# Choosing experts in two batches, with two tiles' rows computed by ScalarE and GpSimd

## The reference

```
x = x + merged @ w_out
t = rms_norm(x, norm_ffn_g)
g_logits = t @ w_router_group + b_router_group          # 4 groups
g_sel = argmax(g_logits);  g_w = softmax(g_logits)[g_sel]
e_logits = (t @ w_router_expert + b_router_expert)[g_sel]   # 4 experts in the group
top_v, top_i = top_k(e_logits, 2);  top_w = softmax(top_v) * g_w
for e in range(16):                                     # combine: the two weights, else 0
    hid = silu(t @ w_gate[e]) * (t @ w_up[e])           # 1024 -> 512
    y += combine[:, e] * (hid @ w_down[e])
return final_rms_norm(x + y)
```

## Time and profile before

| What | Value |
|---|---|
| median of 3 runs | 842.87 us (841.27 to 843.12) |
| the profiled execution's own time | 843.01 us |
| its span, first to last instruction | 841.2 us |
| granted TensorE clock, mean | 0.993 |
| TensorE busy | 819.5 us of the span |
| from the last product of w_out to the first product of the experts | 513.95 to 535.46 us |

### The profile page before, as it was taken

How to read it: one execution, slowest core, us unless ns; L and a number is a source line. 1 busy time by engine, 2 the same in 40 slices (tenths; PEclk the granted TensorE clock), 3 DMA queues, 4 the chain that set the end, 5 groups by cost and what they waited for, 6 DMA issues and landing times.

```text
span 841.2 us, 15813 instructions
## 1 busy us (share of the span) xinstructions
PE 819.5 (97%) x5363; PEld 747.1 (89%) x5363; DVE 589.1 (70%) x957; ACT 512.4 (61%) x935; POOL 88.4 (11%) x77
## 2 busy tenths in 40 slices
PE   9999999999999999999999999999999999999992
PEld 8999999999999998999998888888888888888881
DVE  7383233687778767466457126899989999989995
ACT  7344214567666656554634233588888888888884
POOL 0000000000000000000000001122233322223112
PEclk9999999999999999999999999999999999999997
DMA  8541222233123312332335745799999999999924
GB/s 250 123 146 57 79 68 74 68 109 89 45 81 108 86 44 92 105 99 75 101 101 195 265 165 188 254 371 376 380 375 372 364 371 365 368 366 368 345 69 192
DMA packets 135817, 163.02 MB, mean 194 GB/s; under 512 B 18584, under 2 KB 103704, under 8 KB 135772
## 3 DMA queue, kind: packets, MB, share of 16 engines
q1 hardware_dynamic: 129674, 149.53, 52.7%
q0 software_dynamic: 5952, 12.82, 5.4%
q10 hardware_dynamic: 146, 0.07, 0.0%
HBM read 151.09 MB, written 20.12 MB: 204 GB/s over the span
## 4 chain that ended last, share of the span: by engine, by line
PE 53%; DVE 3%; DMA 2%; issue 1%; ACT 1%; POOLq 0%; POOL 0%; ACTq 0%
PE ps L1767 15%; PE ps L1769 15%; PE ps L1768 15%; PE ps L2219 2%; PE ps L2131 1%; DMA xg<-sum_rows,idi 1%; PE ps L2138 1%; PE ps L2241 1%; DMA sum_rows<-yb,ydn 1%; PE ps L2123 0%; PE ps L2164 0%; PE ps L2165 0%; PE ps L2062 0%; DVE wl L1153 0%; PE ps L1990 0%
## 5 line engine op out<-in xcount | busy, mean ns | idle before, releaser
L1642 DVE TENSOR_TENSOR wl<-rawM,wh 128x1024 fp32r<-128x1024 f32 x189 | 223.9, 1219 | 14.4 <-ACT wh L989 14.2
L989 ACT ACTIVATE wh<-rawM 128x1024 fp32r<-128x1024 f32 x192 | 195.6, 1055 | 6.7 <-PE ps L1769 3.7
L1767 PE MATMUL ps<-hTh,wh 128*128 128x272 f32 (+2 forms) x440 | 129.2, 294 | 1.5 <-ACT qkv L813 1.0
L1769 PE MATMUL ps<-hTh,wl 128*128 128x272 f32 (+2 forms) x440 | 127.4, 290 | 0.0
L1768 PE MATMUL ps<-hTl,wh 128*128 128x272 f32 (+2 forms) x440 | 126.8, 288 | 0.0
L1767 PE MATMUL ps<-wh,xh 128*128 128x256 f32 (+1 forms) x384 | 124.7, 325 | 0.3 <-DVE xl L1688 0.3
L1769 PE MATMUL ps<-wh,xl 128*128 128x256 f32 (+1 forms) x384 | 122.0, 318 | 0.0
L1768 PE MATMUL ps<-wl,xh 128*128 128x256 f32 (+1 forms) x384 | 122.0, 318 | 0.0
L1767 PE MATMUL ps<-wh,hTh 128*128 128x384 f32 x256 | 90.0, 352 | 0.2 <-DVE mA L1273 0.2
L1769 PE MATMUL ps<-wh,hTl 128*128 128x384 f32 x256 | 86.4, 337 | 0.0
L1768 PE MATMUL ps<-wl,hTh 128*128 128x384 f32 x256 | 86.2, 337 | 0.0
(11 more groups left out here) (331 smaller groups left out, 1715.0 us busy)
## 6 DMA issues: line engine op xcount, KB each, us to landing
rawM<-in_w_expert_up SPq DMA_DIRECT2D x64, 512.0 KB, 10.1
rawM<-in_w_expert_down SPq DMA_DIRECT2D x64, 512.0 KB, 8.6
rawM<-in_w_expert_gate SPq DMA_DIRECT2D x64, 512.0 KB, 9.0
rawA<-in_w_in SPq DMA_DIRECT2D x64, 192.0 KB, 3.1
rawA<-in_w_in SPq DMA_DIRECT2D x20, 512.0 KB, 5.3
rawA<-in_w_attn_branch SPq DMA_DIRECT2D x8, 512.0 KB, 3.5
rawA<-in_w_out SPq DMA_DIRECT2D x8, 512.0 KB, 4.3
x<-in_x_prompt SPq DMA_DIRECT2D x4, 512.0 KB, 6.0
```

Source lines behind the costliest of these rows:

```text
L989: nc.scalar.activation(wh[:, (c + 1) % S, :], rawM[:, slot, :], ACT.Copy).then_inc(m_hi, 1)
L1642: V.tensor_tensor(wl[:, sl, :], rawM[:, slot, :], wh[:, sl, :].bitcast(F32), ALU.subtract).then_inc(m_lo, 1)
L1767: T.matmul(out, sh, mh_, start=start, stop=False, **kw)
L1769: return T.matmul(out, sl, mh_, start=False, stop=stop, **kw)
```

## The change

Tiles 0 to 2 in order (AHEAD = 3) are now chosen as soon as their logits are there, while TensorE still works on the last two steps of w_out; the last two tiles follow as a second batch, in the same functions with a slice of tiles. `picked` is an array of its own. The position products of the second batch get a PSUM place of their own, and four products that carry the first batch's counts over run ahead of the second choice. The lists' products are split the same way. New waits go with it: the last two logits products wait until VectorE has read what is in their bank (`lg_read`), `place` of the first batch waits for the last square (item_hot has moved into that space), and the two last tiles' rows take another way: ScalarE scales them (`scale_rows`, after `scale_done`), then GpSimd multiplies with the gain, and stores them. The IDLE counts change, and two operations of `tail_lists` move ahead, the rest of it behind the first split rows.

```diff
-        IDLE = (3, 2, 24, 8, 5, 0, 9)
+        IDLE = (0, 2, 12, 3, 5, 0, 9)
...
@@ GpSimd, for each tile i @@
+                if i >= AHEAD:
+                    pool.wait_ge(scaled_done, i - AHEAD + 1)
+                    pool.tensor_tensor(hb[:, i % 2, :], hb[:, i % 2, :], gb[:], ALU.mult).then_inc(h2_done, 1)
                 pool.wait_ge(h2_done, i + 1)
...
@@ ScalarE @@
+            def scale_rows(i):
+                act.wait_ge(scale_done, i - AHEAD + 1)
+                act.wait_ge(y_out[i % 2], 16 * (i // 2))
+                nc.scalar.activation(hb[:, i % 2, :], x[:, ORDER[i], :], ACT.Copy, scale=rsx[:, i:i + 1]).then_inc(scaled_done, 1)
...
+                if s == 2 * NT - 2:
+                    scale_rows(AHEAD)
             m_hi_split(2, 0, 2, 0, first=True)
+            scale_rows(NT - 1)
...
@@ VectorE @@
+            add_half(NT + 2)
+            normal_rows(1)
+            m_lo_split(0)
+            normal_rows(2)
+            add_half(NT + 3)
+            dve.wait_ge(lg_mm, NT + AHEAD)
+            finish_logits(ahead)
+            select(ahead)
+            row_scale(AHEAD)
+            m_lo_split(1)
+            dve.wait_ge(lg_mm, 2 * NT - 1)
+            finish_logits(slice(AHEAD, NT - 1))
+            add_half(NT + 4)
+            list_values(ahead)
+            dve.wait_ge(ach, 3 * NT)
+            place(ahead, 0)
             row_scale(NT - 1)
...
-            normal_rows(NT - 1, scaled=True)
...
+            select(late)
+            list_values(late)
+            place(late, 1)
...
+            for part, ts in enumerate((ahead, late)):
+                ins = V.scalar_tensor_tensor(out=keep[:, ts], in0=positions[part][:, :, EXPERTS - 1], scalar=float(P),
+                                             in1=picked[:, ts, EXPERTS - 1], op0=ALU.is_lt, op1=ALU.mult)
...
-            tail_lists()
...
             m_lo_split(2)
+            tail_lists()
...
@@ TensorE @@
+                if s >= 2 * NT - 2:
+                    pe.wait_ge(lg_read, s - 2 * NT + 3)
...
+            lists(slice(0, AHEAD), 0)
             idle_products(IDLE[2], 2, *chunk)
...
+            lists(slice(AHEAD, NT), 1).then_inc(ls_mm, 1)
```

More of the change, by code:

```diff
@@ L246, in build @@
         order = r5("order", [P, NT, EXPERTS])
+        picked = r5("picked", [P, NT, EXPERTS])
         assert r5.pos[0] <= 203 * K, r5.pos[0]
@@ L1521, in _ @@
             dve.wait_ge(gb_in, 32)
[L1522 to L1537, removed]
+            gl, el = lg[:, :, 0:EG], lg[:, :, EG:20]
@@ new lines, in place @@
+            def place(ts, part):
+                n = ts.stop - ts.start
+                dve.wait_ge(pos_mm, part + 1)
+                pos = positions[part].unsqueeze(1).broadcast_to([P, 2, n, EXPERTS])
+                c, k_, j_, g_ = chosen[:, :, ts, :], pk[:, :, ts], pj[:, :, ts], ge[:, :, ts, :]
+                link(V.tensor_tensor(c, c, pos, ALU.mult))
+                link(V.tensor_reduce(k_, c, AX.X, ALU.add))
+                link(V.tensor_tensor(g_[:, :, :, 0:4], kt(k_, 4), row(C_STEP, 4, n), ALU.is_ge))
+                link(V.tensor_reduce(j_, g_[:, :, :, 0:4], AX.X, ALU.add))
+                link(V.scalar_tensor_tensor(out=k_, in0=j_, scalar=float(-P), in1=k_, op0=ALU.mult, op1=ALU.add))
+                link(V.tensor_tensor(g_, kt(j_, TILE_COLS), row(C_TILE, TILE_COLS, n), ALU.is_equal))
+                V.tensor_tensor(item_hot[:, :, ts, 0, :], kt(g_[:, :, :, 0], EXPERTS), oht[:, :, ts, :], ALU.mult)
+                for k in range(2):
+                    ins = V.tensor_tensor(slot_hot[:, k, ts, :], pk[:, k, ts].unsqueeze(2).broadcast_to([P, n, P]),
+                                          cst[:, C_SLOT:C_SLOT + P].unsqueeze(1).broadcast_to([P, n, P]), ALU.is_equal)
+                    ins.then_inc(hot_done, 1)
@@ L1559, in _ @@
[L1559 to L1564, removed]
@@ L2172, in _ @@
                     logits_half(s - 1)
+            ones, tri = cst[:, C_ONE:C_ONE + P], cst[:, C_TRI:C_TRI + P]
+            flat = picked[:].rearrange("p t e -> p (t e)")
+            position = ps[:, 6, 192:192 + AHEAD * EXPERTS]
+            position_late = ps[:, 0, 0:(NT - AHEAD) * EXPERTS]
+            es = lambda first, last: slice(first * EXPERTS, last * EXPERTS)
+            more = dict(skip_group_check=True)
+            pe.wait_ge(sel_done, 1)
+            T.matmul(position, tri, flat[:, es(0, AHEAD)], start=True, stop=False, **more)
+            for d in range(1, AHEAD):
+                ins = T.matmul(position[:, es(d, AHEAD)], ones, flat[:, es(0, AHEAD - d)], start=False, stop=d == AHEAD - 1, **more)
+            ins.then_inc(pos_mm, 1)
             idle_products(IDLE[0], 2, *chunk)
@@ L2186, in _, with lists @@
-            ins.then_inc(pos_mm, 1)
+            for first, last, to in ((1, 3, 0), (2, 3, 0), (0, 2, 0), (0, 1, 1)):
+                T.matmul(position_late[:, es(to, to + last - first)], ones, flat[:, es(first, last)], start=first == 1, stop=False, **more)
+            def lists(ts, part):
+                for k in range(2):
+                    pe.wait_ge(hot_done, 2 * part + k + 1)
+                    for t in range(NT)[ts]:
+                        ins = T.matmul(ps[:, 5, 0:FIRST], slot_hot[:, k, t, :], item_hot[:, k, t, 0, TAIL:],
+                                       start=(part == k == t == 0), stop=(k == 1 and t == NT - 1))
+                return ins
```

112 lines of the change are left out of this document (59 added, 53 removed).

## The result

The changed kernel takes 856.91 us (median of four runs, 852.72 to 857.88); the kernel before, run beside it, 842.61. The ratio is 1.0163, with a 95% interval of 1.0132 to 1.0193: slower by some 14 us, where 849.0 with an upper end of 853.4 was forecast. The profiled execution took 856.53 us, its span is 854.7 us. Three executions took 856.5 to 857.9 us at a mean granted clock of 0.978 or 0.979, one 852.72 us at 0.984.

The account below looks back on a forecast made before the run. VectorE's serial chain ahead of the experts was taken to bound the kernel. 843.0 - 0.7 (schedule) + 4.1 (GpSimd holding VectorE) + 2.7 (code switch) = 849.1, so 849.0 us, slower; range 843.9 to 853.4.

Parts of the forecast that it names:

- What bounds the kernel, and where: Router stage ahead of the experts: VectorE's serial chain decides when the experts start, and everything behind moves with them.
- VectorE's schedule, -0.7: Router stage: choosing in two batches leaves a smaller late batch, so the first expert product comes about 0.7 us earlier.
- Exclusion, +4.1: Router stage: GpSimd's two multiplications each hold a two-input VectorE operation, +2.0 and +2.1 us; bounds 0 and 5.2.
- The duration estimated at 2.2 us: Each GpSimd multiplication of 128x1024: 1.30 for a broadcast plus 0.88 for a second input; bounds 0.9 and 2.7 us.
- Rival (1): Only the code switch at the start costs; GpSimd's multiplications run beside VectorE: 844.9 us, chance 0.22.
- (2): Only GpSimd's holding of VectorE in the router stage costs, the code switch being quick: 846.3 us, chance 0.14.
- (3): GpSimd multiplies beside VectorE and the switch is hidden, so the second batch's shorter tail decides: 842.2 us, chance 0.19.
- The code switch, +2.7: Program start: GpSimd's code switch makes broadcast and first tile 3.4 us late, about 0.7 absorbed; bounds 0 and +7.1.
- The 7 us: Length taken for GpSimd's code switch, between transfer landings at 6.0 and 8.1 us; bounds 1.4 and 11.4 us.
- The 6 us switch with its 1.7 us: Range's lower end: a 6 us code switch alone, costing 1.7 us at the start, gives 843.9 us.
- Rival (4): Router stage: TensorE's clock falls between 514 and 520 us; 12 idle products 2.8 us longer, 1.1 hidden; no own chance.
- Fewer idle products cost nothing by themselves: Router stage: 12 idle products at 0.23 us are 2.8 us and end at 523, ahead of the second choice.

Follow-up runs that it names:

- mixed kernel: Changed kernel, one-column GpSimd broadcast added late in the experts, TensorE's gaps filled with idle products, some of them between the small products: 846.30 us, ratio 1.0043.
- code put back: Changed kernel plus one more GpSimd partition broadcast of a single column, read by nobody, late in the experts: 850.83 us, ratio 1.0090.
- the two experiments: Kernel before plus a one-column GpSimd multiplication behind the broadcast: 848.88 us; changed kernel plus a one-column broadcast late in the experts: 850.83 us.
- the copy: Changed kernel with GpSimd's two multiplications by the gain replaced by copies of the same 1024 columns onto themselves: 847.82 us, ratio 1.0056.
- the kernel before with a gap: Kernel before with 12 in place of 24 idle products ahead of the choice, nothing else: median 844.84 us, ratio 1.0022.
- 15 and 26: Changed kernel, one-column GpSimd broadcast added late in the experts, 15 idle products ahead of the last transposes and 26 ahead of the second choice: 848.59 us.

## Why the prediction was wrong

- **What bounds the kernel, and where: right in the main.** The experts' stretch is 306.2 us against 305.7; its start decides. It does not move quite unchanged: in the traces of the changed kernel and its variants it is 305.5 to 307.1 us, once 308.5, on average some 1 us more than in those of before and its variants (305.0 to 306.2). What makes this 1 us is open.
- **VectorE's schedule, -0.7: right.** The second choice ends at 534.30; less the 5.9 us of the start this is 528.4, and 524.2 + 4.1 were forecast. The mixed kernel's stage, 24.96 - 4.24 - 21.51, gives -0.8. What the change is for is therefore there, but is only 0.8 us.
- **Exclusion, +4.1: right**, in mechanism, place and size: 4.24. The duration estimated at 2.2 us is 2.34 and 2.35 (half of the clearing's 1.81 us is 0.9, not 0.88, which leaves the 2.2 as it is). Rival (1) is out by the stalls, (2) by the start, (3) by both.
- **The code switch, +2.7: there, but mis-sized.** The 7 us were the author's estimate from the landing times of transfers; that a switch is a transfer no run shows, nor what happens in it. 8.9 us passed from the MODIFY_POOL_CONFIG row to the broadcast. It starts at 9.93 where the program's last such row is the multiplication's, and at 2.37 where it is a broadcast's again (code put back), as at 2.33 in the kernel before; in the other kernels with a switch at the start the broadcast begins between 9.72 and 10.50. The first transposes start 4.8 us late behind a tile that is 5.67 late, so 0.9 was absorbed as forecast; but TensorE had stood idle for 5.18 us, and its clock of 0.50 under the transposes (1.94 us in place of 1.03) used it up. The term is 5.9 in the trace, 6.9 and 6.1 us in the two experiments, inside its bounds of 0 to 7.1, and 3.2 more than was put in the sum. The 6 us switch with its 1.7 us, from which the range has its lower end, no run shows: the measured ones are those 5.9, 6.9 and 6.1 us. From the row to the broadcast it is 8.9 us at the start, and 8.0 late in the execution (800.4 to 808.4, with GpSimd idle for the last 7.7). In the middle the switch (37 ns rows at 513.7) hides behind ScalarE, as forecast, which releases the multiplication at 520.68: the multiplication starts 0.82 us behind the last product of w_out, and the copy, which has no such row, 0.79.
- **The clock: the step that failed.** Rival (4) was named, was given no chance of its own, was priced at 2.8 - 1.1 = 1.7 us and was left out of the sum. The prediction says that it is in the upper end, but 842.9 - 0.7 + 7.1 + 4.1 = 853.4 holds nothing for it. The step that let it slip is "Fewer idle products cost nothing by themselves", which takes their length at the full clock (0.23 us each; the twelve took 0.44). The prediction had moved the last addition 1.15 + 2.0 us back and had noted that TensorE has little but small products there; it did not ask what TensorE does in these 3.45 us. And it priced one group of idle products, not the 14 idle products, ten list products and eight transposes between the lists and the experts. Measured: 28.64 - 24.96 = 3.7 us in this kernel, of which 2.8 lie behind the lists, and up to 8.2 in the kernel before with a gap.

The sum with measured terms: 843.0 - 0.7 + 4.2 + 5.9 + 3.6 (the rest of the stage) + 0.5 (experts) = 856.5, the profiled execution's 856.53. It has to come out, since the 3.6 is what remains of the stage; that it is the clock rests on the experiments, and on the one execution at a higher mean clock (0.984), which took 852.72. The forecast of 849.0 was short by 3.2 us at the start, 3.6 us of clock and 0.5 us in the experts. The range missed it by the clock: its upper end took 7.1 us for the start, more than the 5.9 measured, and both stalls, but nothing for the clock; with the 1.7 us of rival (4) it would have been 855.1, still short of 856.9.

## What to carry to other kernels

Where a change moves TensorE's input later, look for the stretch in which TensorE then stands idle or has only small products, and price everything behind it at the clock that was measured there, 0.50, idle products first: here they took 0.44 us each in place of 0.23, and in the kernel before with a gap 22 of them held the chain for 9.9 us in place of 5.1. Look through a whole execution for GpSimd operations with a MODIFY_POOL_CONFIG row ahead: here a second kind of them cost 6.1 to 6.9 us at the start of the next execution, unless the first kind came once more behind it. And a multiplication or copy handed to GpSimd did not run beside VectorE where VectorE worked on two SBUF operands; most of its length was lost (2.1 of 2.3 us each for the multiplications, 0.8 of 1.04 for the copies).

## What the hardware showed that was not expected

- A plain GpSimd copy of 1024 columns holds a VectorE operation of 20 columns until its end (0.93 us in place of 0.18); beside a clearing of 2048 columns (1.83 us) VectorE's operations took 0.16 to 0.25 us, as elsewhere.
- What an execution leaves on GpSimd bears on the next: the same broadcast starts at 2.3 to 2.5 us where it is also the program's last operation with a MODIFY_POOL_CONFIG row, and at 9.7 to 10.5 where a multiplication is.
- The same instructions ran at a clock of 1.00 or 0.50 from one execution to the next: the kernel before with a gap of 2.6 us took 842.8 to 850.2 us, where 18 runs of the kernel before itself lie within 841.3 to 844.9. Three executions of such a kernel say little.
- With fewer idle products the clock stayed low from 525 to 548 us without a break; in the changed kernel it came back from 536 to 538 us and again at 545.
- The clock also fell where TensorE had not been idle for more than 0.3 us (at 539 in the changed kernel, at 522 and 532 with 15 and 26); why is open.
